# Seven weight buffers in place of six, and single row and result buffers, in the expert stage of a two-layer transformer kernel

## The reference, cut to what matters

```python
def grouped_expert_mlp(h, expert, weight, w_gu, w_down):
    ...
    def expert_block(args):
        idx, e = args
        gate, up = jnp.split(h_pad[idx] @ w_gu[e], 2, axis=-1)
        return (jax.nn.silu(gate) * up) @ w_down[e]

    y = lax.map(expert_block, (slot_tok.reshape(n_blocks, MOE_BLOCK), block_e))
    y = y.reshape(-1, d) * slot_w[:, None]
    return jnp.zeros((n + 1, d), y.dtype).at[slot_tok].add(y)[:n]
```

## Time and profile before

| | us |
|---|---|
| median of 3 runs (2633.88 to 2638.52) | 2635.58 |
| the profiled execution | 2634.51 |
| its span from the first to the last instruction | 2632.6 |
| expert products of layer 0 | 909.5 to 1459.3 |
| expert products of layer 1 | 2069.2 to 2600.5 |

### The profile page before, as it was taken

The page is one execution under the profiler, slowest core; times in us unless marked ns, Lnnn a source line. Parts: engine busy times, 40 slices in busy tenths (PEclk is TensorE's granted clock), DMA queues, the critical chain, the costliest instruction groups (busy, mean ns, idle before and its releaser), DMA issues.

```text
span 2632.6 us, 33966 instructions
## 1 busy us (share of the span) xinstructions
PE 2505.9 (95%) x12794; PEld 1241.2 (47%) x12794; DVE 1501.1 (57%) x3270; ACT 562.4 (21%) x1181; POOL 457.7 (17%) x527
## 2 busy tenths in 40 slices
PE   6999999999999998999999899999999999999888
PEld 3444456647755533333333344577745433333333
DVE  3264347228778765555555566677787754354435
ACT  3211111118722100000000231488821000000002
POOL 0043200203011132222220012000011122222202
PEclk9999999999999999999999999899999999999999
DMA  9710111114032799999999810300024799999997
GB/s 379 306 26 0 68 49 39 58 22 104 14 142 82 293 392 423 423 382 404 421 408 382 329 49 1 72 2 1 2 75 160 282 402 421 420 413 421 419 406 282
DMA packets 101998, 590.73 MB, mean 224 GB/s; under 512 B 23742, under 2 KB 27078, under 8 KB 76872
## 3 DMA queue, kind: packets, MB, share of 16 engines
q1 hardware_dynamic: 81832, 535.74, 51.7%
q0 software_dynamic: 17408, 43.34, 4.3%
q10 hardware_dynamic: 2592, 9.44, 0.9%
HBM read 555.00 MB, written 45.99 MB: 228 GB/s over the span
## 4 chain that ended last, share of the span: by engine, by line
PE 77%; DMA 14%; DVE 5%; issue 2%; SPq 1%; POOL 0%; ACT 0%; POOLq 0%; DVEq 0%; ACTq 0%
PE PS L2734 28%; PE PS L1072 11%; DMA ar<-in_expert_w_gu_dram 9%; PE PS L1924 5%; PE PS L1268 5%; PE PS L1936 4%; PE PS L1947 4%; PE PS L2157 4%; PE PS L1458 4%; PE PS L1741 4%; DMA ar<-yd 1%; DMA h2d<-ar 1%; PE PS L2150 1%; PE PS L651 1%; DMA ar<-in_ada_w_dram 1%
## 5 line engine op out<-in xcount | busy, mean ns | idle before, releaser
L2734 PE MATMUL PS<-ar 128*32 128x512 f32 (+2 forms) x4608 | 1020.6, 602 | 55.4 <-DMA ar<-in_expert_w_gu_dram 41.9
L2734 PEld LDWEIGHTS PS<-ar 128*32 128x32 f32 (+2 forms) x4608 | 386.3, 138 | 685.5 <-issue 672.2
L1072 PE MATMUL PS<-ar 128*128 128x512 f32 (+1 forms) x768 | 313.9, 565 | 4.2 <-DMA ar<-in_swa_w_in_dram 2.5
L2949 DVE TENSOR_TENSOR ar<-PS,ar 128x512 f32<-128x512 f32 x48 | 33.1, 690 | 485.6 <-ACT ar L2875 485.6
L2963 DVE STREAM_TRANSPOSE ar<-ar 32x128 f32<-32x128 f32 x736 | 296.1, 402 | 10.9
L2875 ACT ACTIVATE ar<-PS 128x512 f32<-128x512 f32 x48 | 28.7, 597 | 1049.8 <-PE PS L2734 1049.8
L1072 PEld LDWEIGHTS PS<-ar 128*128 128x128 f32 x768 | 144.2, 192 | 150.2 <-issue 141.2
L3050 POOL DMA_INDIRECT ar<-h2d,ar x176 | 177.4, 1008 | 140.4 <-DVE ar L2652 57.4
L1980 DVE CUSTOM_DVE_ANT_0 ar<-PS,ar 128x640 f32<-128x640 f32 (+2 forms) x208 | 158.1, 797 | 71.8 <-PE PS L1924 71.7
L2157 PE MATMUL PS<-ar 128*128 128x512 f32 x392 | 175.2, 597 | 1.5 <-ACT ar L2288 0.9
L3058 POOL DMA_INDIRECT yd<-ar x47 | 48.7, 1035 | 711.9 <-DVE ar L2981 699.9
(11 more groups left out here) (349 smaller groups left out, 2452.5 us busy)
## 6 DMA issues: line engine op xcount, KB each, us to landing
ar<-in_expert_w_gu_dram SPq DMA_DIRECT2D x128, 2048.0 KB, 18.2
ar<-in_expert_w_down_dram SPq DMA_DIRECT2D x64, 2048.0 KB, 17.3
ar<-in_ada_w_dram SPq DMA_DIRECT2D x24, 2048.0 KB, 14.7
ar<-yd SPq DMA_DIRECT2D x36, 512.0 KB, 5.6
ar<-in_ab_w_in_dram SPq DMA_DIRECT2D x6, 2048.0 KB, 9.2
h2d<-ar ACTq DMA_DIRECT2D x18, 512.0 KB, 2.8
ar<-in_x_dram SPq DMA_DIRECT2D x8, 512.0 KB, 13.2
ar<-in_ab_w_out_dram SPq DMA_DIRECT2D x1, 4096.0 KB, 30.6
```

What stands on the lines that cost most here:

```text
L1072: mm = nc.tensor.matmul(out_, lhs, rhs, start=(k == 0), stop=(k == KC - 1))
L2734: mm = nc.tensor.matmul(out[at:to], lhsT[:, at:to], w[:, k, cols], start=start, stop=stop)
```

## The change

A seventh 2 MB buffer is made of 16 KB per partition that the expert stage used otherwise. `hb` has one buffer instead of two; `yb` has one, in another place; the gated values overwrite `sg` and `gub` is gone. So:

- gather(b) waits for rows_in(b-1), not for rows_in(b-2); gather(1) waits until TensorE has turned block 0.
- result(b) waits until scatter(b-1) has landed, not scatter(b-2).
- silu(b) waits for gu_in(b-2), not for mul(b-2).
- The plan of pieces has seven buffers, and the first seven are assigned by a table. The d piece of block 1 comes ahead of the g pieces of block 2. In layer 0, piece 1 is loaded before the modulation's first product is done, pieces 2 to 4 after it, piece 5 after its second; in layer 1 one more piece is loaded before the ranking is known.
- The last block's fix-up (`fix_rows`) also waits for the last rows_in.

```diff
-        piece_at = [SLOT1, SLOT1 + 4096, SLOT1 + 8192, SLOT0, SLOT0 + 4096, SLOT0 + 8192]
-        hb = [R(WR + 1024 * i, D) for i in range(2)]
+        piece_at = [SLOT1, SLOT1 + 4096, SLOT1 + 8192, SLOT0, SLOT0 + 4096, SLOT0 + 8192, WR]
+        RING = len(piece_at)
+        TIE = ((0, 1, 3, 6, 2, 4, 5), tuple(range(RING)))
+        FIRST = ((2, 6, 0, 1, 5, 3, 4), (0, 1, 2, 3, 4, 6, 5))
+        hb = R(WR + 4096, D)
...
-        gub = [R(WR + 5120 + 512 * i, 512) for i in range(2)]
...
-        yb = [R(WR + 6144 + 1024 * i, D) for i in range(2)]
+        yb = R(TR, D)
...
-                    q = min(range(6), key=lambda q: (free_at(q), q))
+                    q = FIRST[l][i] if i < RING else min(range(RING), key=lambda q: (free_at(q), TIE[l].index(q)))
...
-                    act.wait_ge(*done(f"{n}_mul", b - 1))
+                    act.wait_ge(*done(f"{n}_guT", b - 1))
...
-                if b >= 2:
-                    dve.wait_ge(*done(f"{n}_yo{b % 2}", 16 * (b // 2)))
-                V.tensor_tensor(yb[b % 2], down_out, row, ALU.mult).then_inc(S(f"{n}_y"), 1)
+                if b >= 1:
+                    dve.wait_ge(*done(f"{n}_yo{(b - 1) % 2}", 16 * ((b + 1) // 2)))
+                V.tensor_tensor(yb, down_out, row, ALU.mult).then_inc(S(f"{n}_y"), 1)
...
             def gather(b):
+                if b >= 1:
+                    pool.wait_ge(*done(f"{n}_tr", 1))
...
             def gather_quarters(b):
-                pool.wait_ge(*done(f"{n}_hbT", b - 1))
+                pool.wait_ge(*done(f"{n}_hbT", b))
...
                 ada_mid_load(sp, 1)
+                moe.load(sp, 1)
                 sp.wait_ge(*done("o0_h2", 2 * nt))
                 ada_mid_rows(sp)
-                for i in (1, 2, 3, 4):
-                    sp.wait_ge(*done("ada_mm", EARLY + 1 + i // 3))
+                for i in range(2, RING):
+                    if i == 2:
+                        sp.wait_ge(*done("ada_mm", EARLY + 1))
+                    elif i == 5:
+                        sp.wait_ge(*done("ada_mm", EARLY + 2))
+                    elif i == 6:
+                        sp.wait_ge(*done("r0_ord", 1))
                     moe.load(sp, i)
```

More of the change, by code:

```diff
@@ L350, in __init__ @@
                 self.l, self.n = l, f"m{l}"
-                self.blocks, self.pieces, self.at, self.fills = moe_blocks(l), [], {}, [0] * 6
+                self.blocks, self.pieces, self.at, self.fills = moe_blocks(l), [], {}, [0] * RING
                 nb, known = len(self.blocks), {}
                 for b in range(nb + 1):
-                    for part, k in (("g", b), ("d", b - 1), ("u", b)) if l == 1 and b == nb - 1 else (("g", b), ("u", b), ("d", b - 1)):
+                    for part, k in (("g", b), ("d", b - 1), ("u", b)) if l == 1 and b == nb - 1 else (("g", b), ("u", b), ("d", b - 1)) if b != 2 else \
+                            (("d", b - 1), ("g", b), ("u", b)):
                         if not 0 <= k < nb:
@@ L363, in __init__ @@
                             self.at.setdefault((part, k), []).append((i, lo, hi))
-                held = [None] * 6
+                held = [None] * RING
                 def free_at(q):
@@ L402, in program @@
         kept = {Moe(1).pieces[i]["buf"] for part in "gud" for i, _, _ in Moe(1).at[part, n_blk[1] - 1]}
-        yg[1] += [[R(piece_at[q] + 2048 * h + 1024 * j, D) for j in range(2)] for q in range(6) if q not in kept for h in range(2)]
+        yg[1] += [[R(piece_at[q] + 2048 * h + 1024 * j, D) for j in range(2)] for q in [q for q in range(RING) if q not in kept][:3] for h in range(2)]
         share(("{}_tr",), "m0", "m1", 2)
@@ L407, in program @@
         share(("{}_hbT", "{}_ga", "{}_gu", "{}_silu", "{}_mul", "{}_guT", "{}_dn", "{}_y"), "m0", "m1", n_blk[0])
-        for q in range(6):
+        for q in range(RING):
             share((f"{{}}_w{q}",), "m0", "m1", 16 * Moe(0).fills[q])
@@ L444, in program @@
         share(("{}",), "rpb_in", "ada_late", 16)
+        share(("{}",), "nv_in", "m0_w6", 16 * (XT + 1))
         share(("{}",), "ada_h0", "masks_in", 16)
@@ L2948, in mul @@
                 dve.wait_ge(*done(f"{n}_gu", b + 1))
-                V.tensor_tensor(gub[b % 2], PS[:, 3, :], sg[b % 2], ALU.mult).then_inc(S(f"{n}_mul"), 1)
+                V.tensor_tensor(sg[b % 2], PS[:, 3, :], sg[b % 2], ALU.mult).then_inc(S(f"{n}_mul"), 1)
             def gu_in(b):
@@ L3013, in block @@
                 dve.wait_ge(*done(f"{o}_act", b + 1))
-                V.tensor_tensor(gub[0], PS[:, 3, :], sg[0], ALU.mult).then_inc(S(f"{o}_dve"), 1)
+                V.tensor_tensor(sg[0], PS[:, 3, :], sg[0], ALU.mult).then_inc(S(f"{o}_dve"), 1)
                 dve.wait_ge(*done(f"{o}_pe", 4 * b + 4))
@@ L3022, in block @@
                 dve.wait_ge(*done(f"{o}_pe", 4 * b + 5))
-                V.tensor_tensor(yb[0], down_out, row, ALU.mult).then_inc(S(f"{o}_y"), 1)
+                V.tensor_tensor(yb, down_out, row, ALU.mult).then_inc(S(f"{o}_y"), 1)
             def first():
@@ L3087, in block @@
                 pool.drain()
-                pool.indirect_dma_start(out=hb[0], out_offset=None, in_=h2d,
+                pool.indirect_dma_start(out=hb, out_offset=None, in_=h2d,
                                         in_offset=bass.IndirectOffsetOnAxis(ap=ocol[:, 0:1], axis=0),
@@ L3108, in moe_sp_all @@
                 ada_mid_load(sp, 1)
+                moe.load(sp, 1)
                 sp.wait_ge(*done("o0_h2", 2 * nt))
                 ada_mid_rows(sp)
-                for i in (1, 2, 3, 4):
-                    sp.wait_ge(*done("ada_mm", EARLY + 1 + i // 3))
+                for i in range(2, RING):
[5 more added lines that the diff above has]
+                        sp.wait_ge(*done("r0_ord", 1))
                     moe.load(sp, i)
             else:
-                for i in (3, 4):
+                for i in range(3, RING - 1):
                     moe.load(sp, i)
-            sp.wait_ge(*done(f"o{l}_h2", 2 * nt))
-            sp.wait_ge(*done(f"r{l}_ord", 1))
-            for i in range(5, len(moe.pieces)):
+                sp.wait_ge(*done("o1_h2", 2 * nt))
+                sp.wait_ge(*done("r1_ord", 1))
+                moe.load(sp, RING - 1)
+            for i in range(RING, len(moe.pieces)):
                 moe.load(sp, i)
-                if i == 6:
+                if i == RING:
                     sp.wait_ge(*done(f"o{l}_r", nt))
@@ L3186, in fix_rows @@
             pool.wait_ge(*done("m1_gu", nb - 1))
+            pool.wait_ge(*done("m1_hbT", nb))
             pool.indirect_dma_start(out=fx_a, out_offset=None, in_=xd, in_offset=bass.IndirectOffsetOnAxis(ap=src_i[:, c:c + 1], axis=0),
```

28 lines of the change are left out of this document (14 added, 14 removed).

## The result

The changed kernel takes 2644.5 us (median of 8 runs, 2641.6 to 2650.6), the kernel before 2635.1 in the same comparison: a ratio of 1.0034, with an interval of 1.0025 to 1.0044. It is 9.4 us slower. The forecast was slower by 26 us: right in sign and in the loop that it described, wrong in size and in what it said of the buffer. The profiled execution of the changed kernel took 2647.2 us, 2.7 above its median.

What follows compares the result with a forecast made beforehand. It took TensorE to bound layer 0 and weight transfers layer 1, with the single buffers' loop becoming the bound. 2634.5 + 21 (layer 0) + 5 (layer 1) = 2660.5, against the median 2661.6, said as 2661 us; range 2630 to 2690.

Steps and rivals of the forecast that it cites:

- the loop: Expert stages: rows_in, four gathers, scatter behind them, landing, result, next rows_in; 24.0 us a turn, at least 20.1.
- 20.0 us for the five transfers: Per block, four gathers and a scatter, first issue to last landing: 19.4 us in the old order, taken as 20.0.
- 23.5 us a block: Layer 1's cycle from result to result, taken just above the 23.1 us that the block's transfers need.
- the buffer's gain: Seventh weight buffer: at most 5.0 us in layer 1 and 10 us in layer 0, hidden since TensorE waits for `y`.
- forecast of +5: Layer 1: result(19) at 2567.8 instead of down(20)'s earlier start at 2562.4, so 5 us slower.
- the other signs: New profile: scatters land in 14 to 15 us, DMA share about 0.95 in layer 0, its first product at about 915.
- result(21) at 1443.0: Layer 0: last result behind a gather, 993.0 + 20 x 22.5; down(22) started before at 1422.4, so +21 us.
- its own bound of 23.1: Layer 1: alternative cycle of 23.1 us, at which the layer changes by -2 us; at 24.0 by +14.
- the tail after it is as before: Behind layer 1's blocks: no change, since the last block's results already waited for all scatters.
- The d piece of block 1 comes sooner: nothing: Weight loads: this piece arrives earlier but nobody waits for it, so it brings nothing.
- The start of layer 0, +6: gather(0) meets a full weights queue and takes 11 us: +6 us, range 0 to +8.
- As long as a block is now: Rival of no change: cycle 21.6 us in layer 0, 23.1 in layer 1; 2633 to 2641 us, say 2636; chance 0.18.

Runs made afterwards that it cites:

- scatter_first: Changed kernel with scatter(b-4) issued ahead of the four gathers of block b on GpSimd, buffers, waits and loads kept: 2633.5 us, ratio 0.9986.
- start_as_before: Changed kernel with layer 0's starting loads timed as before: pieces 1 and 2 wait for the modulation's first product, 3 to 5 for its second: 2642.0 us.

## Why the prediction was wrong in its size

**What failed.** Two steps. The cycle of the loop was priced too long, through 20.0 us for the five transfers, and most of all in layer 1, where 23.5 us a block stood for a measured 22.95. And the buffer's gain was put at nothing, as hidden behind the loop, while the products of layer 1 got 7.3 us shorter. The forecast of +5 there missed by 12.3 us; the start and products of layer 0 missed by 6.2 the same way, and the tail by 4.8 the other.

**What bounds the kernel, and what single buffers do: right.** Every step of the loop is in the trace, the scatter's landing is its last link, and the two lines of scatter_first undo it. Of the other signs, the DMA share in layer 0 was 0.97 (909 to 1290 us) where about 0.95 was forecast, and the first product came at 920.5, or 917.4 less the 3.1 from ahead of the change, where it said about 915.

**"From the first of the five indirect transfers of a block to the landing of all ... I take 20.0": 1 too long.** It was 18.8 us in the turn shown and 19.0 in the median. The 19.4 of the old order held a gap of 1.9 us between the scatter and the first gather (in scatter_first 2176.32 and 2178.22), which the new order doesn't have, since five issues follow each other at 1.3 us. The 0.6 us for "a landing a little behind the last packet" weren't there either.

**Layer 0, result(21) at 1443.0: 1438.1.** First and last of the 21 results:

```profile
992.66 1.23 DVE L2985 TENSOR_TENSOR ar<-PS,ar 128x1024 f32<-128x1024 f32 x1 [8.36 <-DMA yd<-ar]
...
1436.85 1.22 DVE L2985 TENSOR_TENSOR ar<-PS,ar 128x1024 f32<-128x1024 f32 x1 [6.76 <-DMA yd<-ar]
```

Result(1) ended at 993.9 (forecast 993.0, and 3.1 us of that come from ahead of the change). The mean cycle is 444.2 / 20 = 22.2 us against 22.5. Less the 3.1, result(21) is 8.0 us earlier than forecast: 2.2 by result(1), where four gathers took 10.9 us (959.73 to 970.61) and not 13.0, and 5.8 by the 20 cycles. Behind it the stage took 39.2 us to its end, where the forecast had 36.9, and that took 2 back. So +21 became +14.8.

**Layer 1, +5: here the sum failed.** Result(1) and result(19), of the changed kernel and then of the kernel before:

```profile
2153.52 1.23 DVE L2985 TENSOR_TENSOR ar<-PS,ar 128x1024 f32<-128x1024 f32 x1 [8.79 <-DMA yd<-ar]
...
2566.54 1.23 DVE L2985 TENSOR_TENSOR ar<-PS,ar 128x1024 f32<-128x1024 f32 x1 [12.44 <-DMA yd<-ar]
```

```profile
2128.72 1.23 DVE L2981 TENSOR_TENSOR ar<-PS,ar 128x1024 f32<-128x1024 f32 x1
...
2540.73 1.23 DVE L2981 TENSOR_TENSOR ar<-PS,ar 128x1024 f32<-128x1024 f32 x1
2570.41 1.23 DVE L2981 TENSOR_TENSOR ar<-PS,ar 128x1024 f32<-128x1024 f32 x1
```

The cycle is 413.0 / 18 = 22.95 us; before, the mean was 412.0 / 18 = 22.89 (22.90 with six buffers and the loop). The prediction took 23.5, above the 23.1 that the transfers of a block need, though its own bound of 23.1 gave -2; the true value is just below 23.1. The DMA engines are as full as before (1.00, 420 GB/s):

```profile
2158.00:2505.00 347.00, 323.90 (x1038) 128.98 (x1036) 156.35 (x296) 9.15 (x16) 78.33 (x78) 0.99 1.00 420
```

So the transfers stayed the bound, and the loop only spreads their time: before, results came 20.8 us apart in the short blocks and 29.7 in the long ones (2540.73 to 2570.41), now 22.4 to 23.9, while the pieces run ahead. After result(19) the old kernel needed 63.8 us to result(22), the new one, with its weights there, 49.1. From the start of the stage, result(19) came at 483.2 us (2567.8 - 2084.6), 15 earlier than the forecast's 498.6 (2567.8 - 2069.2): 5.4 of it by result(1), ahead of which the four gathers of block 3 took 10.2 us (2121.53 to 2131.68) and not 13.0, and 9.9 by 18 cycles 0.55 shorter. The queues were not full at those gathers (DMA share 0.88 to 0.93 from 2110 to 2140), which may be why they were fast.

**"The 5 to 10 us that the buffer would bring are hidden": not all.** In layer 1 the products got 7.3 us shorter, and in all eleven kernels with seven buffers they took 522.3 to 527.2 us, in the three with six 528.9 to 532.2. Against that stands **"the tail after it is as before"**: +4.8, through the last results, which now wait for each other's scatters, and through the clock (last section). The reason given, that the last block's results waited for all scatters before too, left out that those scatters would be later. "The d piece of block 1 comes sooner: nothing" was right, but the sentence ahead of it, that a piece moving before the ranking is the gain, was not.

**The start of layer 0, +6: +7.9.** The wait for the gather was as priced (6.78 us); the rest is the clock: in the changed kernel the first gate took 8.28 us and the turning ahead of it 1.97, in start_as_before 7.13 and 1.16 (above, and the last section).

**The rivals.** "As long as a block is now" came nearest in mechanism: in layer 1 it is what happened, while layer 0 went as the forecast had it, some 70% as far. Its time of 2633 to 2641 us was still too low. The range, 2630 to 2690, holds 2644.5, but it leaned on a point 17 us too high.

## What to carry over

A buffer taken from a small, latency-bound side path (rows in, results out) turns that path into a loop: add up its links and set them against the time of a block, stage by stage. Where the stage is bound by transfers, a loop that is shorter than the transfers of a block cost nothing here (22.95 us against 23.1), however many waits bear its name; in layer 0, where the blocks took 21.8 us before, the same loop cost 10 to 15 us. And if single buffers are wanted, put in order what shares their queue: the transfer that is ready first goes first, which here was worth 11 us.

## What the runs showed of the hardware

Under a full weights queue the five indirect transfers of a block took a median 18.9 to 19.0 us from first issue to last landing, with the scatter behind four gathers or between them, and a scatter came in 11.0, 12.5 or 13.6 us after its issue with none, two or four gathers ahead (medians of layer 1).

The clock was an effect I had not priced. Windows of the changed kernel around the start of layer 0's products (PEclk is the third number from the end):

```profile
908.00:909.00 1.00, 1.00 (x14) 0.29 (x8) 0.97 (x2) 0.00 (x0) 0.00 (x0) 0.50 1.04 442
911.00:912.00 1.00, 0.00 (x0) 0.00 (x0) 0.03 (x1) 0.00 (x0) 0.00 (x0) 1.00 1.04 434
914.00:915.00 1.00, 0.00 (x0) 0.00 (x0) 0.00 (x0) 0.00 (x0) 0.00 (x0) 0.50 1.05 442
922.00:923.00 1.00, 1.00 (x2) 0.34 (x1) 0.97 (x5) 0.00 (x0) 0.00 (x0) 0.50 1.04 442
924.00:925.00 1.00, 1.00 (x4) 0.48 (x3) 0.00 (x0) 0.00 (x0) 0.00 (x0) 1.00 0.98 414
```

And of start_as_before at the same place:

```profile
905.00:910.00 5.00, 4.88 (x64) 1.67 (x56) 4.83 (x7) 0.00 (x0) 1.71 (x1) 0.72 0.77 284
910.00:915.00 5.00, 3.54 (x14) 2.00 (x15) 4.53 (x6) 0.00 (x0) 0.99 (x1) 1.00 0.89 320
```

In both the granted clock is low at first over the short modulation products, and full by their end. In start_as_before, with a wait of 1.13 us behind them, it stays full. In the changed kernel it falls during the wait of 6.78 us to 0.50, which is the lower of its two levels, 1.2 GHz; the turning and the first part of the first gate run at that level, and the full clock is back from 923. A wait can cost more than its length: here 8.28 - 7.13 + 1.97 - 1.16 = 2.0 us more.

The same shows at the end of layer 1, where the first products of the closing combination wait for `yd`, here in the changed kernel and then in the kernel before:

```profile
2613.32 2.05 PE L3260 MATMUL PS<-ar,cst 128*128 128x512 f32 x2 [4.83 <-DMA ar<-yd]
2615.16 3.62 PE L3262 MATMUL PS<-ar 128*128 128x512 f32 x4
```

```profile
2601.91 1.10 PE L3246 MATMUL PS<-ar,cst 128*128 128x512 f32 x2 [1.41 <-DMA ar<-yd]
2602.85 1.88 PE L3248 MATMUL PS<-ar 128*128 128x512 f32 x4
```

The wait is 3.4 us longer and the clock from 2615 to 2620 is 0.56 in the mean, so that these six matmuls take 2.6 us longer as well (5.25 from the first of them to the next one behind, against 2.65).
